# A deep transformer kernel on one Trainium2 core: GpSimd sums all conditioning slabs in the first mixer, and the first FFN's first part is computed by seven products

## The reference

```python
c_act = jax.nn.silu(c)
for layer in range(2):
    mod = c_act @ ada_w[layer] + ada_b[layer]          # (1, 6 * 1024)
    shift_m, scale_m, gate_m, shift_f, scale_f, gate_f = split(mod, 6)
    h = rmsnorm(x, norm_mix_g[layer]) * (1 + scale_m) + shift_m
    y = gdn_mixer(h, ...) if layer == 0 else mla_mixer(h, ...)
    x = x + gate_m * y
    h = rmsnorm(x, norm_ffn_g[layer]) * (1 + scale_f) + shift_f
    x = x + gate_f * (silu(h @ w_gate[layer]) * (h @ w_up[layer])) @ w_down[layer]
```

## Time and profile before

| | us |
|---|---|
| median of 3 runs | 2347.99 |
| lowest and highest | 2346.89, 2348.34 |
| the profiled execution | 2345.04 |
| its span | 2343.2 |
| PE busy in it | 2260.5 |
| DVE busy | 1398.4 |
| ACT busy | 1043.2 |
| POOL busy | 365.3 |

### The profile page before, as it was taken

One profiled execution on the slowest core, in us unless ns is written; L12 is line 12 of the kernel. 1 busy time (PEld: TensorE's weight loads), 2 busy tenths in 40 slices (PEclk: granted clock), 3 DMA queues, 4 the chain that ended last, 5 costly groups with the idle time before them and its releaser, 6 DMA issues.

```text
span 2343.2 us, 34790 instructions
## 1 busy us (share of the span) xinstructions
PE 2260.5 (96%) x14301; PEld 1913.7 (82%) x14301; DVE 1398.4 (60%) x1800; ACT 1043.2 (45%) x1569; POOL 365.3 (16%) x164
## 2 busy tenths in 40 slices
PE   6999999999999999999999999999999999999998
PEld 4777888788889986668998998888777788998897
DVE  4756755543347765546883676645467345984484
ACT  4546554443215444435552455334355325553352
POOL 0246447347790000000000000000000000000000
PEclk9999999999999999999999999999999999999999
DMA  7333232334452324311333232212211222233232
GB/s 310 135 109 136 102 133 91 121 115 180 183 209 90 109 72 163 128 68 56 109 108 112 87 126 101 87 70 72 90 55 57 87 90 73 91 109 126 90 109 90
DMA packets 40762, 260.56 MB, mean 111 GB/s; under 512 B 4432, under 2 KB 6832, under 8 KB 10416
## 3 DMA queue, kind: packets, MB, share of 16 engines
q1 hardware_dynamic: 40624, 258.59, 30.6%
HBM read 256.42 MB, written 2.15 MB: 110 GB/s over the span
## 4 chain that ended last, share of the span: by engine, by line
PE 78%; DVE 8%; ACT 6%; issue 2%; POOL 2%; DMA 0%; DVEq 0%; ACTq 0%
PE D L301 10%; PE D L303 10%; PE D L302 10%; PE D L1638 7%; PE D L1640 7%; PE D L1639 7%; PE D L1403 2%; PE D L2887 2%; PE D L1405 2%; DVE lo L366 2%; PE D L1404 2%; PE D L2889 1%; PE D L2888 1%; PE D L1422 1%; ACT hi L362 1%
## 5 line engine op out<-in xcount | busy, mean ns | idle before, releaser
L366 DVE TENSOR_TENSOR lo<-raw,hi 128x2048 fp32r<-128x2048 f32 (+3 forms) x131 | 289.1, 2207 | 198.0 <-ACT hi L362 197.8
L362 ACT ACTIVATE hi<-raw 128x2048 fp32r<-128x2048 f32 (+3 forms) x131 | 230.1, 1756 | 326.3 <-PE D L303 239.9
L301 PE MATMUL D<-hH,lo 128*128 128x512 f32 x560 | 227.4, 406 | 7.4 <-DVE lo L366 7.4
L303 PE MATMUL D<-hH,hi 128*128 128x512 f32 x560 | 220.9, 394 | 0.0
L302 PE MATMUL D<-hL,hi 128*128 128x512 f32 x560 | 220.8, 394 | 0.0
L1638 PE MATMUL D<-tH,lo 128*128 128x256 f32 x768 | 216.3, 282 | 0.5 <-issue 0.5
L1640 PE MATMUL D<-tH,hi 128*128 128x256 f32 x768 | 216.3, 282 | 0.0
L1639 PE MATMUL D<-tL,hi 128*128 128x256 f32 x768 | 216.2, 282 | 0.0
L375 POOL TENSOR_TENSOR adar<-adar 128x1024 f32<-128x1024 f32 (+2 forms) x120 | 211.6, 1763 | 9.4
L373 POOL TENSOR_TENSOR adar<-adar,small 128x2048 f32<-128x2048 f32 x40 | 154.2, 3856 | 326.4 <-DVE zi L1289 185.5
L1638 PE MATMUL D<-hH,lo 128*128 128x256 f32 x576 | 162.5, 282 | 2.3 <-ACT D L1721 2.3
(11 more groups left out here) (546 smaller groups left out, 5446.3 us busy)
## 6 DMA issues: line engine op xcount, KB each, us to landing
raw<-in_slabs SPq DMA_DIRECT2D x185, 1024.0 KB, 4.8
adar<-in_ada SPq DMA_DIRECT2D x42, 1024.0 KB, 4.8
fw<-in_ada SPq DMA_DIRECT2D x6, 1024.0 KB, 22.4
x<-in_xin SPq DMA_DIRECT2D x2, 1024.0 KB, 8.8
dt<-bcast SPq DMA_DIRECT2D x8, 256.0 KB, 3.2
dtb<-bcast SPq DMA_DIRECT2D x8, 256.0 KB, 3.5
qd<-bcast SPq DMA_DIRECT2D x8, 256.0 KB, 4.0
out<-x SPq DMA_DIRECT2D x8, 256.0 KB, 2.2
```

Of the source, the lines that this page charges most:

```text
L301: T_.matmul(o, lo[s.slot][:, w], H[:, k, :], start=(k == 0), stop=False)
L303: last = T_.matmul(o, hi[s.slot][:, w], H[:, k, :], start=False, stop=(k == kc - 1))
L362: S_.activation(hi[s.slot][:, 0:n], raw[s.slot][:, 0:n], ACT.Copy).then_inc(hi_ready, 1)
L366: V_.tensor_tensor(lo[s.slot][:, 0:n], raw[s.slot][:, 0:n], hi[s.slot][:, 0:n], ALU.subtract).then_inc(lo_ready, 1)
```

## The change

All 40 conditioning slabs are taken before the first FFN: nine in each pair of the first mixer and four beside the four output slabs. POOL's last add writes its result to a buffer of its own, `adas`, from which PE reads; POOL waits ahead of it until PE has done the sum before. `load_ada` now waits for POOL's sum of the slab two before in place of PE's products. POOL waits for `xx` at its start only. The first FFN is computed by `quick_pe`, `quick_act` and `quick_dve` like the others, and ACT waits there for the last sum ahead of the differences, since their buffers lie over `adar`.

```diff
-ADA_P = 5
+ADA_PAIR = (9, 9, 9, 9)
...
+        adas = sb("adas", [P, 1, 2 * P], scope=gdn)
...
-            for n in (4, 2, 1):
-                last = nc.gpsimd.tensor_tensor(r3[:, 0:n], r3[:, 0:n], r3[:, n:2 * n], ALU.add)
-                if n > 1:
-                    chain.link(last)
-            last.then_inc(ada_sum, 1)
+            for n in (4, 2):
+                chain.link(nc.gpsimd.tensor_tensor(r3[:, 0:n], r3[:, 0:n], r3[:, n:2 * n], ALU.add))
+            if a.b > ADA0:
+                pool.wait_ge(ada_done, a.plus(0))
+            nc.gpsimd.tensor_tensor(adas[:], r3[:, 0:1], r3[:, 1:2], ALU.add).then_inc(ada_sum, 1)
...
+            pool.wait_ge(gg["xx"], 2)
+            for a in range(ADA0, 2 * ADA_L - ADA_SKEW):
+                ada_chunks(pool, chain, Slab(a))
...
-                                 adar[a.slot][:, m * P:(m + 1) * P], ones[:, 0:1], start=True, stop=True)
+                                 adas[:, 0, m * P:(m + 1) * P], ones[:, 0:1], start=True, stop=True)
...
-            if a.b >= 2:
+            if a.b >= ADA0 + 2:
+                sp.wait_ge(ada_sum, a.plus(-1 - ADA0))
+            else:
                 sp.wait_ge(ada_done, a.plus(-1))
...
+                if p:
+                    ada_at(0)
                 w("kn", p + 1)
...
-                    if lv in ((3, 4, 5, 6) if p else (2, 3, 4, 6)):
-                        ada_at(lv - 3 if p else min(lv - 2, 3))
+                    if p or lv > 1:
+                        ada_at(lv if p else lv - 2)
...
-                    if t == (2 if p else 1):
-                        ada_at(4)
+                    if t == 0:
+                        ada_at(7 if p else 5)
+                    elif t == 2:
+                        ada_at(8 if p else 7)
+                    elif p == 0:
+                        ada_at(6 if t == 1 else 8)
...
+            if f == 0:
+                act.wait_ge(ada_sum, 2 * ADA_L - 8)
...
+                load_slab(sp, Slab(8 + 3 * p if p else 7), SEQ.get(8 + 3 * p if p else 7))
+                for _ in range(3):
+                    load_ada(sp, Slab(next(a)))
...
                     load_slab(sp, Slab(10 + 3 * p), SEQ[10 + 3 * p])
+                for k in a:
+                    load_ada(sp, Slab(k))
...
-            ffn_pe(pe, G_FFN0, 0, 2, 1, ADA0 + GH // 2 * ADA_P)
+            quick_pe(pe, G_FFN0, 0, 1)
```

More of the change, by code:

```diff
@@ L592, in ones_half, with final_pe @@
             last.then_inc(fss_ready, 1)
-        def final_pe(pe, base, kc, H, L, ready, f, begun=False):
+        def final_pe(pe, base, kc, H, L, ready, f, begun=False, also=lambda j: None):
             for j in range(N_OUT - 1):
                 s = Slab(base + j)
+                also(j)
                 if j == 0 and not begun:
@@ L604, in final_pe @@
             for h in range(2):
+                also(N_OUT - 1 + h)
                 for m in range(2):
@@ L1448, in gdn_pe @@
                 qp = qs[p % 2]
-                ada_at = lambda j: ada_pe(pe, Slab(ADA0 + ADA_P * p + j))
+                ada_at = lambda j: ada_pe(pe, Slab(ADA0 + sum(ADA_PAIR[:p]) + j))
                 lv_fill = 3 if p in (0, 3) else 2
@@ L1617, in build @@
         N7 = ((N_GUA - NORD) // 2, N_GUB // 2)
-        Q7 = lambda f, part: 2 * (N7[1] + (f - 1) * sum(N7) + part * N7[0])
-        RUN = lambda f, part: 2 * f + part - 1 if f else 0
+        Q7 = lambda f, part: 2 * (f * sum(N7) + part * N7[0])
+        RUN = lambda f, part: 2 * f + part
         quarter = lambda t_: t_[:].rearrange("p (a k m n) -> p a k m n", a=2, k=4, m=2)
@@ L1995, in quick_dve @@
             final_dve(dve, g + 2 * N7[1], gate, 2 * f + 1)
[L1998 to L2011, removed]
-            final_pe(pe, base + N_GUB, FB, aH, aL, hidden(FA // 2, {1: close}), n)
@@ L3149, in _ @@
             for p in range(GH // 2):
-                a = ADA0 + 2 + ADA_P * p
+                a = iter(range(ADA0 + 2 + sum(ADA_PAIR[:p]), ADA0 + 2 + sum(ADA_PAIR[:p + 1])))
                 front = p + 1 < GH // 2
+                if p:
+                    load_ada(sp, Slab(next(a)))
                 if front:
@@ L3193, in alone @@
                     load_slab(sp, Slab(g + n - 1))
-            ada1 = ADA0 + GH // 2 * ADA_P
+            ada1 = ADA0 + 2 + sum(ADA_PAIR)
             load_slab(sp, Slab(G_GOUT + 2))
+            load_ada(sp, Slab(ada1))
             load_slab(sp, Slab(G_GOUT + 3))
-            load_ada(sp, Slab(ada1))
             load_ada(sp, Slab(ada1 + 1))
-            load_slab(sp, Slab(G_FFN0))
-            load_slab(sp, Slab(G_FFN0 + 1))
-            left = 2 * ADA_L - ADA_SKEW - ada1 - 2
-            both(G_FFN0 + 2, ada1 + 2, left // 2, 2, (1, 1))
-            g = G_FFN0 + 2 + left
-            alone(g, G_MLA - g)
+            alone(G_FFN0, G_MLA - G_FFN0)
             for p in range(GH // 2):
@@ L3240, in _ @@
             gdn_pe(pe)
-            final_pe(pe, G_GOUT, KC, hH, hL, h_batch(pe, 1), 0)
-            ffn_pe(pe, G_FFN0, 0, 2, 1, ADA0 + GH // 2 * ADA_P)
+            final_pe(pe, G_GOUT, KC, hH, hL, h_batch(pe, 1), 0, also=lambda j: ada_pe(pe, Slab(ADA0 + sum(ADA_PAIR) + j - 1), 1) if j else None)
+            quick_pe(pe, G_FFN0, 0, 1)
             mla_in_pe(pe)
@@ L3286, in _ @@
             close_act(act, G_GOUT, 0, 1, col(mod, MD(0, 3)))
[L3287 removed]
+            quick_act(act, G_FFN0, 0, 1)
             close_act(act, G_MIN - N_OUT, 1, 2, col(mod, MD(1, 0)))
```

95 lines of the change are left out of this document (8 added, 87 removed).

## The result

The changed kernel takes 2439.19 us (median of 4 runs, 2433.62 to 2442.95) against 2347.44 in the same comparison: a ratio of 1.0394, 95% interval 1.0382 to 1.0406, slower by 92 us. The forecast was 2416 with a range of 2392 to 2438. So the direction and the main mechanism were right, and the size was 23 us short, 1 us outside the range.

A forecast was written before the change was run, and what follows sets the result against it. TensorE was taken to bound the kernel, with no slack for new waits in the mixer. -19.3 + 7.2 + 72.0 + 7 - 4 + 5 = +67.9 us on 2345.0 gave 2412.9, plus 3.0 for the median: 2416 us, range 2392 to 2438.

The forecast's parts named there:

- The FFN part: First FFN's first part: 249.8 us falls to 230.6 us with seven products, -19.3 us.
- The stalls: First mixer: PE waits for sums whose loads stand behind weight-slab loads in SP's queue, +72.0 us.
- (a): First mixer: POOL and DVE hold each other up when they meet, +7 us, bounds 0 and 25.
- (c): First mixer: granted clock halves after stalls, 0 to 14 us for eight; +5 taken for three pair starts.
- The price of 15.5 us: First mixer: time from a weight-slab load's issue to POOL's sum of the conditioning slab behind it.
- (b): First mixer: PE's existing idle time is absorbed by stalls, 0 to -9 us, taken as -4.
- Sixteen visits: PE taking conditioning sums in the mixer, 0.36 us each; with four beside the output slabs, +7.2 us.
- (d): Output stage: POOL has sums 36 to 39 ready in time, 0 us, upper bound 6.
- The rule on an exclusive lock: GpSimd and two-SBUF-input VectorE steps lock shared ports per instruction; would put (a) some 15 us higher.
- The fourth: Rival: clock falls in every stall and meetings reach their upper bound, 9 and 18 us more, 2443 us; chance 0.08.
- The first rival: Mixer stalls don't come and the kernel gets faster, -12.1 us, 2336 us; chance 0.06.
- The second: Rival: only POOL's pace binds, 84 us a pair, 6 us in all, 2342 us; chance 0.03.

The follow-up runs named there:

- e2: Kernel before with only the first FFN's first part changed, its twenty conditioning slabs left out: 2323.9 us.
- e5: Changed kernel with SP's load list for the mixer in another order, nothing added or removed: 2359.3 us.
- e3: Changed kernel with PE doing 18 to 50 extra products ahead of its wait at the nine long stalls: 2429.6 us.
- e4: Changed kernel with POOL's product and first two adds left out for the last six conditioning slabs (wrong result): 2429.9 us.
- e9: e5 with POOL's product and first two adds left out for all 40 slabs (wrong result): 2333.0 us.
- e7: e5 with POOL waiting, ahead of conditioning slab 37, for DVE's last hL of the mixer (a gate): 2356.4 us.
- e8: e7 with a second buffer for POOL's sums: 2353.7 us.
- e11: e8 without the gate ahead of slab 37, POOL's product cut into four and its first add into two: 2371.8 us.
- e1: Changed kernel with POOL itself issuing conditioning loads from the third slab on, each after its own sum: 2386.4 us, ratio 1.0169.

## Why the prediction was nearly right and not quite

- **The FFN part: right.** 230.4 us (230 to 231 forecast), and as much alone in e2. The gain is 19.4 us, where 19.3 were counted.
- **The stalls: right, nearly place by place.** The terms were 13.3 + 3.3 for the end of pair 0 and the start of pair 1, where 14.7 (11.4, and 1.1 and 2.2 at the two visits ahead of it) and 0.3 were measured. Then 7.6 and 6.1 in pair 1: 7.5 and 7.8. In pair 2 8.2, 7.6 and 6.1: 9.4, 7.8 and 8.7. In pair 3 8.2, 7.6 and 4.0: 8.1, 4.5 and 6.6. The sum is 75.3 and was 72.0. With term (a), +7, it was to be 79, so (a) as extra waiting for POOL came to 3.3 us. The list has nine blocked places, while (c) counts eight and the lower bound of the range seven; nine came. The mechanism is shown by e5, which takes 66.5 us of the 75.3 away by the order of issues alone. The price of 15.5 us is 15.8 in the rows.
- **Term (b), absorbed idle time: right.** PE's idle time in the mixer rose from 8.75 to 80.3 us; less 75.3 that leaves 5.0, so 3.7 us were absorbed and -4 was taken. The 4 was picked between 0 and 9, and that it came so near is luck.
- **Term (c), the granted clock: the step that failed.** The prediction has "I take +5 for the three starts of a pair", with an upper bound of 14. The runs show 22.8, by the difference of busy times. PE's busy time in the mixer rose by 29.8 us. Sixteen visits at 0.44 us are 7.0 of it (a shift of 0.44 to 0.45 at each is seen where nothing waits; I had 0.36), which leaves 22.8 for products at half speed. It lies between e3's rough estimate of 18 and the bound of 25. Two assumptions were wrong. The fall came with each of the nine long stalls (4.5 to 11.4 us), once behind two short ones near 172, and once more in the output stage: eleven stretches, not three. And six of them lasted 10.2 us; behind the nine long stalls they went on for 4 to 7, where I had priced the 3.5 us of the earlier trace rows. That next visits would wait anyway and hide it was wrong too: the waits came out at 75.3 and not 79, so 4 us at most were hidden. The likely reason, which no run tests, is that POOL's sums follow loads that wait for DVE's splits, and DVE waits for the slowed products.
- **Term (d), the output stage at 0, bound 6: the second step that failed.** It was 10.6 us: 1.8 the four visits (counted, as 1.4), 6.2 waits and 2.6 the clock behind them. I asked whether POOL would have its sums in time, and it did (no visit there waits). I did not ask what POOL does to DVE in the last steps of the mixer, where DVE's gated steps and `hL` are the path to the first output product. e4 took 9.3 us away by making POOL idle there. The rule on an exclusive lock that I had set beside (a) would have told me to look, but I had used it to price the wrong side: POOL's pace, not DVE's lateness.
- **The rivals.** The fourth ("the clock falls in every stall and the meetings stand at their upper bound", 2443 us) was nearest to 2439 and got 0.08. Its clock part came out still larger than it said, its meetings at another place. By the Trainium skill, "TensorE: Matmul & The Clock Gate", section "HAM oscillation — how this bites in real kernels", each wait for a DMA between bursts of products brings the half clock back anew; the trace agrees, with 11 stretches at 0.5 in the mixer and behind it, one with each of the nine long stalls. I should have given that rule more than 0.08. The first rival, 2336 us, is nearly met, but only in e9, with POOL's work left out. The second (only POOL's pace binds, 2342 us) had pace and meetings as 84 us a pair. In e5, which comes closest to that case, the mixer is 22.7 us longer and not 12: it counted what meetings cost POOL, and nothing of what they cost DVE or of the clock.

Summed up from the rows: forecast of the mixer 5.8 + 72 + 7 - 4 + 5 = 85.8, measured 101.4; of the output stage 1.4, measured 10.6. Within the mixer the clock makes +17.8 of the difference, the visits +1.2, and and the waits, 3.7 below 79, take some back. Those two differences, 15.6 and 9.2 us, are the miss of 24.8 in the profiled execution; the medians lie 23.2 apart.

Left open: how e9's gain over e5 in the mixer divides between POOL's pace, DVE's lateness and the clock; the 4 us by which e2's median lies lower than its stages say; and whether e7 and e8 gained at all.

## What to carry to other kernels

In a queue that waits for semaphores in order, price each load from the moment the load *ahead* of it may go, and merge the lists by the times at which the buffers come free: here an order of issues was worth 80 us, and the change behind it at best 12 (e9, with most of POOL's work left out). Here a stall of PE cost its own length and then some microseconds at half clock; with nine stalls of 8 us, that was nearly another third of them. When GpSimd gets more work, ask not only whether it keeps pace, but also what it does to VectorE's steps on the path.

## What the runs showed of the hardware

Where both inputs of a DVE step are in SBUF, a meeting with POOL looks like a block until the other's instruction ends, and not like a sharing. In e8 one DVE step of 128 x 8 elements began 0.06 us after POOL's product and took as long as that (DVE's row, then POOL's):

```profile
455.56 3.57 DVE L784 SCALAR_TENSOR_TENSOR gsc<-mod,vec 128x8 f32<-128x8 f32 x1
```

```profile
455.50 3.60 POOL L374 TENSOR_TENSOR adar<-adar,small 128x2048 f32<-128x2048 f32 x1 [7.94 <-DVE hL L1266]
```

The same step took 0.17 us in e5, where POOL was idle. In the Trainium skill, "SBUF — State Buffer", section "SBUF: two separate sides", the shared ports are an exclusive lock that the engine which starts first holds for its whole instruction; the trace agrees, for a step as small as 8 columns.

Not every step of DVE is held up. In e8 four that take one of their tensors from PSUM (`D`) started beside a product of POOL and took 0.75 to 0.77 us each, as they do in e9 with POOL idle (0.75). The splits, which read two SBUF tensors, took 3.0 us on average in e8 and 2.29 in e9. DVE's rows, then POOL's:

```profile
172.84 0.75 DVE L1180 TENSOR_SCALAR vs<-D,vec 128x512 f32<-128x512 f32 x1
173.63 2.32 DVE L1182 SCALAR_TENSOR_TENSOR vs<-D,vec,vs 128x511 f32<-128x511 f32 x3
```

```profile
172.83 3.60 POOL L374 TENSOR_TENSOR adar<-adar,small 128x2048 f32<-128x2048 f32 x1
```

So it is the steps between SBUF tensors (splits, gated steps, `hL`) that POOL's work should be kept away from.

Cutting POOL's product to quarters and its first add to halves gave DVE 31 us back and cost POOL 31 (e11). What also surprised me was the length of the stretches at half clock: 4 to 7 us beyond the end of each long stall, in which products of 512 columns took 0.63 us and not 0.39. Issuing a 1 MB load from POOL's own list took 0.59 us and 0.30 of waiting ahead of it (e1), and the loads then landed in 5.1 us in the median, against 6.9 from behind SP's slab loads.
